# Feed-forward layers: VectorE takes the remainders of the weight sums from SBUF instead of from a copy in PSUM

## The reference, cut to what matters

```python
def swiglu(h, w_gate, w_up, w_down):
    return (jax.nn.silu(h @ w_gate) * (h @ w_up)) @ w_down
```

## Time and profile before

| | us |
|---|---|
| median of 3 runs | 1660.84 |
| lowest and highest | 1658.45 and 1662.52 |
| the profiled execution | 1661.55 |
| its span in the profile | 1659.7 |
| TensorE busy in it | 1630.0 |
| VectorE busy | 1259.7 |
| ScalarE busy | 851.8 |
| GpSimd busy | 520.2 |

### The profile page before, as it was taken

How to read it: one execution, slowest core, us unless ns; L and a number is a source line. 1 busy time by engine, 2 the same in 40 slices (tenths; PEclk the granted TensorE clock), 3 DMA queues, 4 the chain that set the end, 5 groups by cost and what they waited for, 6 DMA issues and landing times. The chain is left out here.

```text
span 1659.7 us, 27549 instructions
## 1 busy us (share of the span) xinstructions
PE 1630.0 (98%) x10695; PEld 1452.8 (88%) x10695; DVE 1259.7 (76%) x1752; ACT 851.8 (51%) x1314; POOL 520.2 (31%) x368
## 2 busy tenths in 40 slices
PE   9989999999999999999999999999999999999997
PEld 8867889999998866789998998888898999899886
DVE  7767788845876799888855886678968985488675
ACT  6448457733763312557733774443335673377342
POOL 1452135503540336325602550111402560255000
PEclk9999999999999999999999999999999999999999
DMA  6310224443433565233344333422222334333432
GB/s 223 97 51 2 77 77 114 110 115 96 121 106 104 125 146 145 93 83 102 103 114 114 102 94 114 133 78 77 77 76 78 102 103 115 114 102 93 124 95 83
DMA packets 284923, 169.11 MB, mean 102 GB/s; under 512 B 8336, under 2 KB 278880, under 8 KB 284800
## 3 DMA queue, kind: packets, MB, share of 16 engines
q1 hardware_dynamic: 283792, 165.16, 35.3%
q0 software_dynamic: 720, 1.72, 0.3%
q10 hardware_dynamic: 288, 0.54, 0.1%
HBM read 156.71 MB, written 2.10 MB: 96 GB/s over the span
## 5 line engine op out<-in xcount | busy, mean ns | idle before, releaser
L1113 PE MATMUL ps<-act,w 128*128 128x512 f32 x788 | 306.0, 388 | 6.5 <-POOL w L564 2.3
L1115 PE MATMUL ps<-act,w 128*128 128x512 f32 x788 | 299.7, 380 | 0.0
L1114 PE MATMUL ps<-act,w 128*128 128x512 f32 x788 | 299.7, 380 | 0.0
L1460 PE MATMUL ps<-act,w 128*128 128x256 f32 x2160 | 266.5, 276 | 2.6 <-DVE w L2138 1.3
L1460 PEld LDWEIGHTS ps<-act,w 128*128 128x128 f32 x2160 | 253.8, 192 | 6.9 <-DVE t L2209 1.9
L645 ACT ACTIVATE w<-raw 128x2048 fp32r<-128x2048 f32 (+2 forms) x102 | 162.7, 1595 | 187.3 <-PE ps L1115 173.8
L1809 DVE TENSOR_TENSOR w<-raw,w 128x2048 fp32r<-128x2048 f32 (+2 forms) x93 | 180.4, 1940 | 40.0 <-ACT w L645 39.9
L482 POOL TENSOR_TENSOR raw<-raw 128x512 f32<-128x512 f32 x60 | 80.6, 1343 | 391.7 <-DVE sqacc L1829 163.0
L1113 PE MATMUL ps<-hid_hi,w 128*128 128x512 f32 x528 | 200.1, 379 | 0.0
L1114 PE MATMUL ps<-hid_lo,w 128*128 128x512 f32 x528 | 200.1, 379 | 0.0
L1115 PE MATMUL ps<-hid_hi,w 128*128 128x512 f32 x528 | 200.1, 379 | 0.0
(11 more groups left out here) (423 smaller groups left out, 3027.6 us busy)
## 6 DMA issues: line engine op xcount, KB each, us to landing
raw<-in_ffn_w_gate_dram SPq DMA_DIRECT2D x44, 512.0 KB, 4.0
raw<-in_ffn_w_up_dram SPq DMA_DIRECT2D x44, 512.0 KB, 5.2
raw<-in_w_gate_upffn_dram SPq DMA_DIRECT2D x44, 512.0 KB, 4.6
raw<-in_ffn_w_down_dram SPq DMA_DIRECT2D x32, 384.0 KB, 4.2
raw<-in_conv_w_pw_dram SPq DMA_DIRECT2D x24, 512.0 KB, 5.8
raw<-in_w_in_dram SPq DMA_DIRECT2D x24, 512.0 KB, 4.6
raw<-in_ffn_w_down_dram SPq DMA_DIRECT2D x32, 320.0 KB, 3.6
z<-z SPq DMA_DIRECT2D x30, 262.0 KB, 4.9
```

What stands on the lines that cost most here:

```text
L1113: pe.matmul(out, lhs[0], rhs[0], start=start, stop=False)
L1114: pe.matmul(out, lhs[0], rhs[1], start=False, stop=False)
L1115: return pe.matmul(out, lhs[1], rhs[0], start=False, stop=stop)
L1460: ins = pe.matmul(out[:, 0:HALF], lhs, rhs, start=start and k == 0 and rhs is b_hi and lhs is w_hi, stop=k == Q4 - 1 and lhs is w_lo, skip ...
```

## The change

ScalarE no longer copies the three sums of a unit to PSUM (line 829, 180 instructions), and the waits for `split_done`, `up_split` and `bank_free` ahead of these copies go with them. The high part (824) now raises `sum_hi`. VectorE's `lo_sum` reads the sum where GpSimd left it, in `ssum` or in `raw`, both in SBUF. No instruction is added, and the order of what is left is the same on every engine.

```diff
-            def hi_sum(u, n, dn, c):
+            def hi_sum(u, n, c):
                 w = seven(u)
                 act.wait_ge(sem("w_sums"), 4 * w + 2 + c)
                 if w:
                     act.wait_ge(sem("up_product"), 6 * (w - 1) + (4, 6, 5)[c])
                 src = ssum[:, c] if c < 2 else raw[:, n % 2, Q4 * P:2 * Q4 * P]
-                act.activation(sw_hi[:, c], src, ACT.Copy)
-                if c == 0:
-                    act.wait_ge(split_done, n)
-                else:
-                    act.wait_ge(sem("up_split"), 3 * w + c)
-                act.activation(sum_bank(dn, c)[:, :], src, ACT.Copy).then_inc(sem("sum_hi"), 1)
+                act.activation(sw_hi[:, c], src, ACT.Copy).then_inc(sem("sum_hi"), 1)
...
                             hi_panel(u, n)
-                            act.wait_ge(bank_free, T0[dn] + 9)
                             for c in range(3):
-                                hi_sum(u, n, dn, c)
+                                hi_sum(u, n, c)
...
-            def lo_sum(u, dn, c):
+            def lo_sum(u, n, c):
                 ve.wait_ge(sem("sum_hi"), 3 * seven(u) + 1 + c)
-                ve.tensor_tensor(sw_lo[:, c], sum_bank(dn, c)[:, :], sw_hi[:, c].bitcast(F32), ALU.subtract)\
+                src = ssum[:, c] if c < 2 else raw[:, n % 2, Q4 * P:2 * Q4 * P]
+                ve.tensor_tensor(sw_lo[:, c], src, sw_hi[:, c].bitcast(F32), ALU.subtract)\
                     .then_inc(sem("up_split") if c < 2 else split_done, 1)
```

More of the change, by code:

```diff
@@ L274, in seven @@
             return u - 2 * (u // KF) - 2
-        def sum_bank(dn, c):
-            return bank(T0[dn]) if c == 1 else ps[4]
         def up_banks(dn, u):
@@ L892, in ffn @@
                             cast_hidden(u - 1)
-                            hi_sum(u + 1, n + 1, dn, 0)
-                            hi_sum(u + 1, n + 1, dn, 1)
+                            hi_sum(u + 1, n + 1, 0)
+                            hi_sum(u + 1, n + 1, 1)
                             continue
@@ L897, in ffn @@
                             take(u, dn, 0)
-                            hi_sum(u, n, dn, 2)
+                            hi_sum(u, n, 2)
                             silu(u - 1)
@@ L910, in ffn @@
                         if not first:
-                            hi_sum(u, n, dn, 1)
+                            hi_sum(u, n, 1)
                         take(u, dn, 0)
                         if not first:
-                            hi_sum(u, n, dn, 2)
+                            hi_sum(u, n, 2)
                         if k < ks[-1]:
@@ L2256, in ffn @@
                             low_hidden(u - 1)
-                            lo_sum(u + 1, dn, 0)
+                            lo_sum(u + 1, n + 1, 0)
                             low(flat2(combo("T3")[1]), flat2(tt3[:, :, :]), flat2(combo("T3")[0]), "bt_hi", 4 * f + 3,
@@ L2261, in ffn @@
                         if k == 2:
-                            lo_sum(u, dn, 1)
+                            lo_sum(u, n, 1)
                             whole_gate(u - 1, n - 1)
-                            lo_sum(u, dn, 2)
+                            lo_sum(u, n, 2)
                             whole_hidden(u - 1)
@@ L2275, in ffn @@
                             for c in range(2):
-                                lo_sum(u, dn, c)
+                                lo_sum(u, n, c)
                             hidden(u - 1, n - 1)
-                            lo_sum(u, dn, 2)
+                            lo_sum(u, n, 2)
                         if k < ks[-1]:
@@ L2301, in ffn @@
                             for c in range(3):
-                                lo_sum(u + 1, dn, c)
+                                lo_sum(u + 1, n, c)
                         else:
```

## The result

The changed kernel takes 1702.28 us (median of 5 runs, 1701.02 to 1703.04) against 1660.84 before (5 runs, 1658.45 to 1662.52); the ratio is 1.0247 with a 95% interval of 1.0236 to 1.0258. It is slower by some 41 us, and 1700.5 was forecast. The profiled execution took 1702.40 us with a span of 1700.6. In the changed kernel's text line 2144 has become 2135, 2138 is 2128, 2219 is 2210, 2209 is 2200, 2216 is 2207, 2203 is 2194, 2238 is 2229; on GpSimd 482, 486, 490, 492 are 478, 482, 486, 488, and ScalarE's 824 and 815 are 820 and 811.

The account below looks back on a forecast made before the run. TensorE bounds the kernel before; afterwards VectorE's chain of waits, blocked by GpSimd, does. Three layers of 13.3 us, less 0.9, give +39 on 1661.55: 1700.5 us, range 1680 to 1714.

Parts of the forecast that it names:

- TensorE is full, VectorE has 0.4 us a round: TensorE busy 98% of the span; line 2209 ends 0.4 us before the fourth product would have to wait for it.
- Two inputs in SBUF are what can be blocked, for up to 1.15 us: A GpSimd instruction keeps a VectorE instruction with both inputs in SBUF out for 1.15 us from its own start.
- The remainder of sum 2 goes behind a GpSimd instruction in nearly each round, 1.11 us: After line 2219, sum 2's remainder no longer slips past a GpSimd instruction but waits behind it: 1.11 us more.
- two theories for the share of the three remainders: Expected for sum 2 alone read from SBUF: two thirds of the loss, +25 to +30 us, or in equal parts +14.
- Rounds of 10.47 and 10.03 us in turn: VectorE's rounds after the change alternate between two lengths, mean 10.25 us against TensorE's 9.38.
- the first kind: Round of 10.47 us: line 482 begins at 1.93; 2219 blocked 0.80, sum 2 1.11, line 2138 1.05 us.
- the sum: Three layers of 13.3 us make 39.9, less 0.9 for earlier stalls: +39 on 1661.55, giving 1700.5 us.
- Part a +7.8, part b +5.5: Loss in each layer's two stretches: part a 7.8 us, part b 5.5 us, first units and longer rounds together.
- ScalarE's dropped copies give nothing of their own: 180 copies of 0.59 us, 106 us of ScalarE in all, gain nothing by themselves since ScalarE isn't the bound.
- Rival 1: Blocks don't add up, as remainders fall into GpSimd's gaps or its burst slides: 1659.6 us; chance 0.06.
- Rival 2: Only sum 2 is behind a GpSimd instruction; rounds 0.1 to 0.5 us over TensorE's, 1670 to 1685 us; chance 0.10.
- Rival 3: Remainders hold up GpSimd, so line 482, panel copy and 2138 come later: 10.9 us rounds, 1725, half 1712; chance 0.06.

Follow-up runs that it names:

- the two partial kernels: Kernel before, with only some remainders read from SBUF and their copies dropped: sums 0 and 1 alone 1671.24 us, sum 2 alone 1685.46 us, beside 1658.47.

## Why the prediction was right

Point by point, by its steps.

- *TensorE is full, VectorE has 0.4 us a round.* It held: blocks beyond that came out as TensorE's waits for line 2209, 29.0 us at the weight loads, whose idle time in the six parts grew by 37 us in all; 35 to 45 were forecast.
- *Two inputs in SBUF are what can be blocked, for up to 1.15 us.* Held, and tested from both sides: without GpSimd's reads line 2219 stays at 414 to 418 ns and the remainders within 678 to 719, and with one input in PSUM line 2203 stays at 424 to 425 and line 2219 at 412 to 416.
- *The remainder of sum 2 goes behind a GpSimd instruction in nearly each round, 1.11 us.* Held in 43 of 60: the median is 1770, which is 0.68 and 1.09. Of the two theories for the share of the three remainders, the unequal one was right, 24 to 27 us for sum 2 alone.
- *Rounds of 10.47 and 10.03 us in turn.* Both kinds are there and take turns, at 10.35 and 9.97, a mean of 10.16 instead of 10.25. In the first kind GpSimd's 478 came 0.1 us earlier in the round, at 1.83 and not 1.93, and line 2207 began 0.15 us later, at 2.10 and not 1.95, so that line 2210 was blocked for 0.54 (0.96 less 0.42) and not 0.80. Over 39 rounds such a mean is 3 to 4 us less than the sum had. But not all rounds are of the two kinds: five take 11.4 us and four others, in the parts b, 10.5 to 10.7. All 42 rounds between the first and the last of each part have a mean of 10.33, over the 10.25 of the sum; in the kernel before they had 9.47. **So that the time came within 2 us of the forecast is in part luck**: the two kinds were taken a little too long, and kinds that the sum did not have made up for it.
- *Part a +7.8, part b +5.5.* Measured 9.0, 6.5, 7.8 and 6.2, 5.3, 5.9. The first layer's part a is over by 1.2, although its rounds of the two kinds are under: two others in it took 11.4 us. The second layer's, which has none of these, is under by 1.3.
- *ScalarE's dropped copies give nothing of their own.* No kernel drops copies without reading the sum from SBUF; where the 60 of sum 0 were dropped the time stayed as it was. With all reads from SBUF the copies' absence gave 6 us (1708.39 against 1702.28; 10 by the parts), at least in part by the 0.5 us that the remainder of sum 1 starts earlier. ScalarE's busy time fell by 85 us and not by the 106 that were forecast: its instructions overlap in the rows by about 0.1 us each, and 180 times 0.59 counts that twice.
- *Rival 1, not slower*, would have needed the remainders to find gaps. Sum 0 does. *Rival 2, half*, 1670 to 1685, is where the two partial kernels lie, 1671 and 1685, and not the whole change. *Rival 3*, GpSimd's first instruction late in each round, shows in single rounds only.

One of the five rounds of 11.4 us, from 328.11 on (line 2128 is the panel's remainder):

```profile
330.89 0.69 DVE L2135 TENSOR_TENSOR sw_lo<-raw,sw_hi 128x512 fp32r<-128x512 f32 x1
334.70 2.88 DVE L2128 TENSOR_TENSOR w<-raw,w 128x2048 fp32r<-128x2048 f32 x1 [3.12 <-ACT w L811]
```
```profile
331.19 1.53 POOL L478 TENSOR_TENSOR raw<-raw 128x512 f32<-128x512 f32 x1 [3.28 <-DMA raw<-in_ffn_w_up_dram]
```

GpSimd's 478 came 7.2 us after the remainder of sum 2 before it (322.18 + 1.77 = 323.95) and not 6.0, because the load took longer. VectorE then is free of blocks but stands idle for 3.12 us behind the panel copy, which waits for 478. The sum had this load, with its semaphores, at a fixed 6.0 us. What makes the four rounds of 10.5 to 10.7 us was not looked into.

## What to carry to other kernels

A copy that looks like waste may be what keeps an instruction with two SBUF inputs away from GpSimd: before dropping one, list which GpSimd instructions that read SBUF run in the same stretch, and who is queued behind VectorE. Durations of one line that spread from the free value to about one GpSimd instruction more are the sign. The cure isn't always a copy: let a result that VectorE makes for itself stay in a free part of PSUM, or put the exposed instruction where the engine would have waited.

## What the runs showed of the hardware that was not expected

- The hold ends before the row does. GpSimd's instruction of 1.28 us kept VectorE out for 1.15 us from its start, in both kernels. The Trainium skill (SBUF — State Buffer, SBUF: two separate sides) speaks of the whole instruction; the measurement decides, and the prediction put the difference at 4 to 14 us in its sum. GpSimd's rows are rough, so the 1.15 rests on VectorE's: it is counted back from their ends by their free durations.
- The 1 MB load of a panel has a second length. Of 66 such loads in the changed kernel, from issue to landing, the 37 during which no packet of the queues of kind instruction was moved took 5.51 to 5.85 us. Of the 29 others, 19 took 5.53 to 6.02 and ten 6.58 to 7.12. All five rounds of 11.4 us have one of these ten. That the packets are what makes a load longer was not tried, and most loads with them are not longer.
